# Two key batches loaded over the first feed-forward's hidden rows, and fewer, longer runs of attention work between the projection's matmuls

## The chip, the cores and the metric

The kernel runs on one NeuronCore of a Trainium2 chip. The metric is the time of one execution on the device, in microseconds (us). Engines run side by side, each in the order of its own program, and wait for each other on semaphores: TensorE (PE) multiplies matrices, VectorE (DVE) and ScalarE (ACT) work on elements, GpSimd (POOL) does a little, and SyncE (SP) issues nearly all DMA transfers from HBM.

## The reference

One inference step of a decoder layer for a prompt of 256 tokens and 8 samples of one token each with 1024 cached keys and values, all in fp32:

```python
x = x + 0.5 * swiglu_ffn(x, ffn1_norm, ffn1_w_in, ffn1_w_out)        # 1024 -> 2 x 2816 -> 1024
proj = rmsnorm(x, mix_norm) @ w_in                                    # u | q | k | v | q_mem, 2048 columns
y_pool = pool_mixer(u, ...)                                           # causal means of 2, 4, 8, 16 tokens
q, k = rotary(rmsnorm(q)), rotary(rmsnorm(k))                         # 8 heads x 64
y_moba = moba_attention(q, k_all, v_all)                              # blocks of 256: best 3 past ones and the own
y_mem  = mem_attention(rmsnorm(q_mem), mk, mv)                        # 4 heads, 256 memory tokens
x = x + concat(y_pool, y_moba, y_mem) @ w_out
x = x + 0.5 * swiglu_ffn(x, ffn2_norm, ffn2_w_in, ffn2_w_out)
```

The samples' keys and values lie in 128-token pages of a paged cache, found through `page_table`: 8 batches of 8 pages of 256 KB for the keys, and as many for the values.

## The kernel before

**Matmuls.** Every big product is split in high and low fp32r parts and done as three matmuls (`three`, L1504): L1506, L1507, L1508. For each weight tile of 512 KB SP loads `raw`, ACT writes the high part `w_hi` (L702), DVE the low part `w_lo` (L1022), and PE uses both. A ring of four such tiles turns: ACT's split of unit n waits until PE has used unit n - 4, and SP's load of unit n until DVE has split unit n - 4. The small products of the attention and all sample work are plain fp32 matmuls or PE transposes.

**The first feed-forward** ends with 22 units of `w_out` (`ffn_out(0)`, L1570): unit k takes hidden row k from `h_hi` and `h_lo`, which take 23 KB a partition each, and the last two units run together (`last_two`, L1599), so they wait for both splits. Meanwhile SP loads these units, the pages of key batch 3, and looks up the page numbers of batches 4 to 7 (`HELD`), 4 per unit at the end (L569 to L580). DVE, after each split, turns a pair of key pages in place (`turn_pair`, L1030): 16 pairs, those of batches 0 to 3, at the splits of units 6 to 21 (L1309). Then come the splits of the projection's units 0 and 1, the residual, and the samples' input `xs` (L1318).

**The projection rows.** The projection `x @ w_in` has 16 weight units, the rows r = 0 to 15: four each for q, k, v and for u with q_mem. Each row is four steps P (`project`, L1609) of three matmuls. All else up to the mixing product `w_out` is hung between the P by a table written by hand, `EXTRA` (L399): `EXTRA[r][i]` lists the tokens that come before the i-th P of row r, or behind it for i = 4; `TAIL` (L423) holds what follows the last row. PE, ACT, DVE all walk the same list (`steps`, L433) and each does its part of a token, so the list sets the order on all three. Tokens that matter here:

- S r: the samples' matmuls of row r from `raw` (L1638, 16 matmuls); ES their evacuation. ET: evacuation of the prompt's projection (`token_evac`).
- K b: the logits of key batch b (`key_logits`, L1653, 32 matmuls L1666). G g: DVE turns page pair g (four pairs a batch). QF: ACT spreads the queries of batches 4 to 7, after K3.
- OWN, A: own key and the softmax of the samples' logits; A3 holds its exponentials, A4 the turns of the probabilities, A5 the own values. V b: the values of batch b (L1940, 64 matmuls).
- NQ, NV, ND, NS, NG, NR: squares (ACT), variances (DVE), roots (ACT), scales, gains, rope (DVE) of a norm. T: turns of prompt queries and keys on PE (L1514) with ACT's evacuation.
- HA, HM, HE, HV, HB, HT, PV: logits, maxima (DVE), exponentials (ACT), scaling (DVE), turns (PE), evacuation (ACT) and values of the prompt's heads, two heads at a time for HA and PV. HY: evacuation of a pair of PV. MG: turns of memory key pages. Y, YR: turns and scaling of the samples' values. M, MK: the memory softmax and logits of the samples.
- W r, WL r: the splits of weight unit r on ACT and on DVE.

**Loads in the rows.** SP walks its own list (L599 to L631): projection units with key batch 4 behind unit 3, batch 5 behind unit 7, then 6, 7, the values, the memory keys and values, and the mixing weights. A batch goes to a slot as soon as the batch that had it is used (`free_wait`, L333). Batch 4 goes to `early_slot`, over the hidden rows, once the feed-forward is done (`w_used` at `U_WIN`).

Of the kernel before, what the change touches and what calls it, by code (L numbers as in the profile page):

```python
# [110 lines left out]
def layer(nc, a):  # L111

    ctx = ExitStack()
    with ctx:
# [99 lines left out]
        at[0] = late_end
        early_slot = place("early_slot", [P, PAGES * 512], at=at[0])
        vp = over("vp", [P, 2, 512])
        up = over("up", [P, 2, 512])
        kT = over("kT", [P, 4, NP])
        prob_pair = over("prob_pair", [P, 2, 2, NP])
        kp = over("kp", [P, 2, 512])  # L220
        probT_pair = [probT_even, over("probT_odd", [P, 2 * NP])]
# [12 lines left out]
        joined = over("joined", [P, 3, P])
        same, repeat, quarter_of = joined[:, 0, :], joined[:, 1, :], joined[:, 2, :]
        own_y = over("own_y", [P, 2, 4, 4])
        v_cols = over("v_cols", [P, P])
# [1763 lines left out]
```

## Time and profile before

| | us |
|---|---|
| median of 3 runs (lowest, highest) | 560.4 (559.86, 560.5) |
| the profiled execution | 560.33 |
| its span, first to last instruction | 558.5 |
| PE busy | 551.9 (99%) |
| DVE busy | 398.8 (71%) |
| ACT busy | 269.4 (48%) |

The stretches of the span that matter here: units 2 to 21 of the first feed-forward's second product end at 215.2 us, the projection rows reach to about 310, the tail to 337.7, and the mixing product and the second feed-forward follow. PE's granted clock is 1.00 of 2.4 GHz in all of them. Matmuls overlap in the pipeline: the start of one to the start of the next is what one costs, and "busy" hides small losses. A bracket behind a row of the timeline is the idle time of that engine ahead of it and the engine and line that ended it.

### The profile page before, as it was taken

The page shows a single profiled execution, that of the slowest core. Times are in us where ns is not written, and L with a number is a line of the kernel's source. Part 1 is how long each engine was busy: PE and PEld are TensorE (multiplying, and loading weights), DVE is VectorE, ACT ScalarE, POOL GpSimd, SP SyncE. Part 2 cuts the span into 40 slices and gives each one's busy share as a digit, 9 for nine tenths or more (in the row PEclk, how much of TensorE's full clock was granted, in tenths as well). Part 3 has the DMA queues.
Part 4 walks back from the last instruction along what each step waited for, and adds up shares of the span by engine and source line. Part 5 has one row for each costly group of instructions (what it writes and reads, how often), then busy time and mean ns, then how long its engine had stood idle before and what let it go on. Part 6 is the DMA issues. An engine that isn't in the chain of part 4 may idle for free.

```text
span 558.5 us, 13391 instructions
## 1 busy us (share of the span) xinstructions
PE 551.9 (99%) x5075; PEld 514.3 (92%) x5075; DVE 398.8 (71%) x715; ACT 269.4 (48%) x425; POOL 17.7 (3%) x24
## 2 busy tenths in 40 slices
PE   9999999999999999999999999999999999999997
PEld 9999999999899998566777779999999999999997
DVE  4686878885688877899936685689777777664444
ACT  6843465444543337344535885475444344433330
POOL 1000000000000003000000000140000000000000
PEclk9999999999999999999999999999999999999999
DMA  8799999784567664899999984567756666465523
GB/s 242 220 262 303 268 316 282 239 248 152 191 217 273 209 205 154 283 344 383 361 315 377 374 301 137 164 179 196 211 171 188 186 171 191 133 226 181 188 75 79
DMA packets 137480, 128.40 MB, mean 230 GB/s; under 512 B 10936, under 2 KB 108879, under 8 KB 137431
## 3 DMA queue, kind: packets, MB, share of 16 engines
q1 hardware_dynamic: 134703, 127.24, 72.6%
q10 hardware_dynamic: 2736, 0.61, 0.5%
q8 instruction: 26, 0.43, 0.3%
q14 instruction: 15, 0.12, 0.1%
HBM read 125.12 MB, written 2.83 MB: 229 GB/s over the span
## 4 chain that ended last, share of the span: by engine, by line
PE 83%; DVE 7%; DMA 5%; ACT 2%; issue 1%; SPq 1%; DVEq 0%; ACTq 0%
PE banks L1506 24%; PE banks L1507 24%; PE banks L1508 24%; DMA raw<-in_ffn_w_in 4%; PE banks L1666 3%; PE banks L1514 2%; PE banks L1940 2%; DVE w_lo L1022 2%; PE banks L1638 1%; PE banks L1867 1%; PE banks L1891 1%; DMA page_ids<-in_page_table 1%; DVE banks L1436 0%; DVE kp L1138 0%; ACT w_hi L702 0%
## 5 line engine op out<-in xcount | busy, mean ns | idle before, releaser
L702 ACT ACTIVATE w_hi<-raw 128x1024 fp32r<-128x1024 f32 x158 | 166.4, 1058 | 195.7 <-PE banks L1508 157.6
L1022 DVE TENSOR_TENSOR w_lo<-raw,w_hi 128x1024 fp32r<-128x1024 f32 x158 | 193.8, 1232 | 74.2 <-ACT w_hi L702 73.2
L1506 PE MATMUL banks<-x_hi,w_hi 128*128 128x264 f32 x752 | 214.1, 285 | 0.2 <-DVE h_tmp L1066 0.2
L1507 PE MATMUL banks<-x_lo,w_hi 128*128 128x264 f32 x752 | 213.0, 283 | 0.0
L1508 PE MATMUL banks<-x_hi,w_lo 128*128 128x264 f32 x752 | 213.0, 283 | 0.0
L1506 PEld LDWEIGHTS banks<-x_hi,w_hi 128*128 128x128 f32 x752 | 141.6, 188 | 0.8 <-issue 0.7
L1507 PEld LDWEIGHTS banks<-x_lo,w_hi 128*128 128x128 f32 x752 | 141.7, 188 | 0.0
L1508 PEld LDWEIGHTS banks<-x_hi,w_lo 128*128 128x128 f32 x752 | 141.0, 188 | 0.0
L1506 PE MATMUL banks<-h_hi,w_hi 128*128 (+1 forms) x352 | 100.2, 285 | 0.1
L1508 PE MATMUL banks<-h_hi,w_lo 128*128 (+1 forms) x352 | 100.1, 284 | 0.0
L1507 PE MATMUL banks<-h_lo,w_hi 128*128 (+1 forms) x352 | 100.0, 284 | 0.0
L1506 PEld LDWEIGHTS banks<-h_hi,w_hi 128*128 128x128 f32 x352 | 66.4, 189 | 0.3 <-ACT mem_kv L880 0.3
L1507 PEld LDWEIGHTS banks<-h_lo,w_hi 128*128 128x128 f32 x352 | 66.4, 189 | 0.0
L1508 PEld LDWEIGHTS banks<-h_hi,w_lo 128*128 128x128 f32 x352 | 66.3, 188 | 0.0
L1066 DVE TENSOR_TENSOR h_tmp<-banks,rstd 128x264 f32<-128x264 f32 x44 | 18.9, 429 | 22.6 <-PE banks L1508 22.6
L1033 DVE STREAM_TRANSPOSE kv<-kv 128x1024 f32<-128x1024 f32 x28 | 33.9, 1228 | 0.0
L1506 PE MATMUL banks<-w_hi,x_hi 128*128 128x512 f32 x64 | 28.0, 438 | 0.3 <-ACT qp L795 0.3
L727 ACT ACTIVATE sg<-sg 128x264 f32<-128x264 f32 x44 | 18.3, 415 | 16.4 <-DVE sg L1061 16.4
L1508 PE MATMUL banks<-w_hi,x_lo 128*128 128x512 f32 x64 | 25.3, 395 | 0.0
L1507 PE MATMUL banks<-w_lo,x_hi 128*128 128x512 f32 x64 | 25.2, 394 | 0.0
L1075 DVE TENSOR_TENSOR h_lo<-h_tmp,h_hi 128x264 f32 (+1 forms) x44 | 19.1, 433 | 3.6
L1071 DVE TENSOR_TENSOR h_tmp<-sg,h_tmp 128x264 f32<-128x264 f32 x44 | 19.0, 432 | 2.8 <-ACT sg L727 1.5
(287 smaller groups left out, 503.9 us busy)
## 6 DMA issues: line engine op xcount, KB each, us to landing
raw<-in_ffn_w_in SPq DMA_DIRECT2D x86, 512.0 KB, 4.8
raw<-in_ffn_w_out SPq DMA_DIRECT2D x44, 512.0 KB, 3.8
kv<-in_cache_k SPq DMA_DIRECT2D x56, 256.0 KB, 4.9
kv<-in_cache_v SPq DMA_DIRECT2D x48, 256.0 KB, 6.3
raw<-in_w_in SPq DMA_DIRECT2D x12, 512.0 KB, 5.7
late_slot<-in_cache_v SPq DMA_DIRECT2D x16, 256.0 KB, 5.3
raw<-in_w_out SPq DMA_DIRECT2D x8, 512.0 KB, 7.2
raw<-in_mem_w_kv SPq DMA_DIRECT2D x4, 512.0 KB, 3.5
```

What stands on the lines that cost most here:

```text
L702: act.activation(w_hi[:, n % RING, :], raw[:, n % RING, :], ACT.Copy).then_inc(hi_ready, 1)
L727: act.activation(sg[:, s, :], sg[:, s, :], ACT.Silu).then_inc(silu_ready, 1)
L1022: vec.tensor_tensor(w_lo[:, n % RING, :], raw[:, n % RING, :], w_hi[:, n % RING, :].bitcast(F32), ALU.subtract).then_inc(lo_ready, 1)
L1033: vec.transpose(key_pair(g), key_pair(g)).then_inc(k_turned8, 1)
L1066: vec.tensor_tensor(h_tmp[:, s, :], bank[b0 + 2 * s + 1][:, 0:N], rstd[:], ALU.mult).then_inc(gu_free, 1)
L1071: vec.tensor_tensor(h_tmp[:, s, :], sg[:, s, :], h_tmp[:, s, :], ALU.mult).then_inc(hm_ready, 1)
L1075: vec.tensor_tensor(h_lo[:, ds(c, 1), :].rearrange("p a n -> p (a n)"), h_tmp[:, s, :], h_hi[:, ds(c, 1), :].rearrange("p a n -> p (a n)") ...
L1506: pe.matmul(out, lhs[0], rhs[0], start=start, stop=False)
L1507: pe.matmul(out, lhs[0], rhs[1], start=False, stop=False)
L1508: return pe.matmul(out, lhs[1], rhs[0], start=False, stop=stop)
L1514: return pe.transpose(out, in_, ident[0:k, 0:k])
L1666: mm = pe.matmul(bank[LG_BANK][32 * hp:32 * hp + 32, half * NP:(half + 1) * NP], q_cols[:, c0:c0 + 32], keys[:, 4 * hp + c], start=(b4 == ...
```

## The change

Seven things change, and no arithmetic:

1. Key batches 4 and 5 (`HIDDEN`) load during the first feed-forward's second product, each page over hidden rows that PE is done with: at units 6, 8, ... 20 SP waits until PE has used two more units, looks up and loads one page of each. 16 pages that were loaded in the rows move here; the lookups of `HELD` (now 6 and 7) are halved and stand at units 18 to 21.
2. DVE turns three pairs ahead of the product (`LEAD_PAIRS`) and the pairs 3 to 23 at the splits of units 6 to 20 (`EARLY_PAIRS`), up to two at a split. The turns of 16 to 19 and 20 to 23 wait for the hidden pages. K0 now waits for all 24 pairs.
3. Batches 6 and 7 load into the slots of 0 and 1 and are turned together (G 24 to G 31 in rows 3 and 4).
4. Key logits, samples, own keys and values are gathered: K0 to K3 together; S4 to S7 with K4, K5; K6, K7 with S8 to S11; S12 to S15 with V3. The logits of a head pair come ahead of the values.
5. Values load in another order: batch 0 waits for K2, batch 1 for K3, batch 2 now stands ahead of unit 14. The mixing weights' first unit, which SP issues ahead of value batch 5, waits for S12 as before, and S12 is now in row 14.
6. `rows`, `rows_x` get a place of their own beside the squares' buffer, so A and N tokens pass each other in other orders: A3 now comes before ND4, NQ5 after HE7. The wait of T2 on K4 becomes a wait of T0 on K5.
7. In the tail WL16 moves behind HV7, and HB10, HB11 ahead of M1.

```diff
-HELD = (4, 5, 6, 7)
+HELD = (6, 7)
+HIDDEN = (4, 5)
+LEAD_PAIRS = (0, 1, 2)
+EARLY_PAIRS = ((3,), (4,), (5, 16), (6,), (7, 20), (8, 17), (9,), (10, 21), (11,), (12, 18), (13,), (14, 22), (15,), (19,), (23,), ())
...
-            if kind == "k" and b == 4:
-                eng.wait_ge(w_used, U_WIN)
-            elif kind == "k" and b > 4:
-                eng.wait_ge(k_used, b - 4)
+            if kind == "k":
+                eng.wait_ge(k_used, b - 5)
             elif kind == "v" and b < 5:
-                eng.wait_ge(k_used, (4, 6, 7, 8, 8)[b])
+                eng.wait_ge(k_used, (3, 4, 7, 8, 8)[b])
...
             for k in range(HT):
                 load_unit(U_OUT1, k, 0, ffn_out[0][:, k:k + 1, :])
+                if k >= 6 and k % 2 == 0:
+                    t = k // 2 - 3
+                    sp.wait_ge(w_used, U_OUT1 + 2 * t + 2)
+                    for b in HIDDEN:
+                        pages[b, t] = page_of(b, t)
+                        load_page("k", b, t)
...
-            load_batch("k", 4)
+            sp.wait_ge(w_used, U_WIN)
...
-            load_batch("k", 5)
+            load_batch("k", 6)
+            load_batch("k", 7)
             load_projection(8)
-            load_batch("k", 6)
             load_projection(9)
-            load_batch("k", 7)
             load_projection(10)
             load_batch("v", 0)
             load_projection(11)
+            load_batch("v", 1)
             load_projection(12)
-            load_batch("v", 1)
             load_projection(13)
+            load_batch("v", 2)
             load_projection(14)
             load_projection(15)
-            load_batch("v", 2)
...
-                    if k == 2:
-                        act.wait_ge(k_used, 5)
+                    if k == 0:
+                        act.wait_ge(k_used, 6)
...
-                kv_wait(vec, "k", g // 4, (g % 4 // 2,))
+                if g // 4 in HIDDEN:
+                    vec.wait_ge(hidden_loaded[g % 4], 16 * 2 * len(HIDDEN))
+                else:
+                    kv_wait(vec, "k", g // 4, (g % 4 // 2,))
...
+            for g in LEAD_PAIRS:
+                turn_pair(g)
             ffn_out_loop(0, 0, 1)
...
-                pe.wait_ge(k_turned8, 4 * (b + 1))
+                pe.wait_ge(k_turned8, 4 * (b + 1) if b in HELD else 4 * HELD[0])
```

The table's change, as the order in which PE meets it (P x n stands for n projection steps). Before:

```
Px4 T5 Px2 S0-3 Px3 QT0 Px3 QT2 SS0 P K0 K1 P K2 K3 P S4-7 Px3 K4 Px3 T0 P K5 P T1 Px5 S8 Px2 K6 Px2 S9 Px4 S10 K7 OWN1
Px2 S11 P A1 Px7 A4 Px2 S12 Px2 A5 T2 P T3 V0 P HA0 S13 V1 Px3 HB0 HB1 P PV0 V2 HA1 S14 Px3 V3 HB2 HB3 P S15 PV1 HA2 V4
P MG0 Y0 P MG1 HB4 HB5 P MG2 P | PV2 HA3 MG3 V5 T4 POOL0 MG4 HB6 HB7 MG5 PV3 MG6 HA4 POOL1 MG7 QT1 V6 HA5 HB8 HB9 MK0
V7 PV4 M1 HB10 HB11 Vmem Y1 PV5 MIX0 ...
```

After:

```
Px4 T5 Px2 S0-3 Px3 QT0 Px3 QT2 SS0 P K0-3 Px2 S4-7 K4 K5 Px8 T0 P T1 Px4 K6 K7 S8-11 OWN1 P A1 Px11 A4 Px7 T2 P T3 A5 P
HA0 V0 V1 Px3 HB0 HB1 P HA1 PV0 V2 Px4 HB2 HB3 P HA2 PV1 V3 S12-15 Px2 Y0 Px2 MG0 HB4 HB5 P MG1 P | MG2 PV2 V4 HA3 V5
MG3 T4 POOL0 MG4 HB6 HB7 MG5 PV3 MG6 HA4 POOL1 MG7 QT1 V6 HA5 HB8 HB9 MK0 V7 PV4 HB10 HB11 M1 Vmem Y1 PV5 MIX0 ...
```

On DVE the stretch that holds the turns of batches 6 and 7 becomes: WL6 G24 to G30 WL7 NR2 G31 NV2 NS2 NV3 NS3 WL8 NG3 WL9 OWN0 A0 OWN1 WL10 A2 NV4.

## Rows read from the trace of the kernel before

**Rows 1.** The page, part 4: who makes up the chain that ended last.

```profile
PE 83%; DVE 7%; DMA 5%; ACT 2%; issue 1%; SPq 1%; DVEq 0%; ACTq 0%
```

**Rows 2.** Stage windows: length, busy time of PE, PEld, DVE, ACT, POOL, clock, DMA share.

```profile
156.10:215.20 59.10, 59.10 (x488) 59.10 (x487) 47.83 (x58) 23.32 (x27) 0.00 (x0) 1.00 0.63 208
215.20:310.40 95.20, 93.93 (x1148) 66.60 (x1146) 73.36 (x184) 45.90 (x100) 5.95 (x7) 1.00 0.98 337
```

**Rows 3.** PE in order of time (start, length, line): a break for sample matmuls.

```profile
219.13 0.39 PE L1506 MATMUL banks<-w_hi,x_hi 128*128 128x512 f32 x1
...
219.92 1.93 PE L1638 MATMUL banks<-raw,xs 128*8 128x128 f32 x64
221.78 0.50 PE L1506 MATMUL banks<-w_hi,x_hi 128*128 128x512 f32 x1
222.12 0.39 PE L1507 MATMUL banks<-w_lo,x_hi 128*128 128x512 f32 x1
222.34 0.39 PE L1508 MATMUL banks<-w_hi,x_lo 128*128 128x512 f32 x1
```

**Rows 4.** PE in order of time: sample matmuls that hand over to key logits.

```profile
263.19 0.62 PE L1638 MATMUL banks<-raw,xs 128*8 128x128 f32 x16
263.63 1.91 PE L1666 MATMUL banks<-kv,q_cols 128*32 128x256 f32 x32
```

**Rows 5.** PE in order of time: a break of four transposes.

```profile
246.12 0.60 PE L1514 MATMUL banks<-ident,qp 128*128 128x128 f32 x4
246.47 0.48 PE L1506 MATMUL banks<-w_hi,x_hi 128*128 128x512 f32 x1
```

**Rows 6.** PE in order of time: four places in the rows where it waits.

```profile
239.83 0.40 PE L1508 MATMUL banks<-w_hi,x_lo 128*128 128x512 f32 x1
240.50 0.48 PE L1506 MATMUL banks<-w_hi,x_hi 128*128 128x512 f32 x1 [0.27 <-ACT qp L795]
...
277.89 0.40 PE L1508 MATMUL banks<-w_hi,x_lo 128*128 128x512 f32 x1
278.44 0.33 PE L1514 MATMUL banks<-ident,v 128*128 128x128 f32 x1 [0.16 <-DVE p_own L1411]
...
288.60 1.15 PE L1514 MATMUL banks<-ident,prob_pair 128*128 128x128 f32 x6
289.50 0.48 PE L1506 MATMUL banks<-w_hi,x_hi 128*128 128x512 f32 x1
...
307.36 0.66 PE L1514 MATMUL banks<-ident,kv 128*128 128x128 f32 x4 [0.58 <-ACT kv L723]
```

**Rows 7.** SP's queue in order of time: a unit, a page, batches of eight pages.

```profile
173.99 0.33 SPq L457 DMA_DIRECT2D raw<-in_ffn_w_out  x1
177.25 0.34 SPq L493 DMA_DIRECT2D kv<-in_cache_k  x1
...
238.71 4.08 SPq L493 DMA_DIRECT2D kv<-in_cache_k  x8
...
294.68 5.81 SPq L496 DMA_DIRECT2D kv<-in_cache_v  x8
```

**Rows 8.** DMA issues, 216 to 345 us: count, KB each, median us to landing.

```profile
kv<-in_cache_k SPq DMA_DIRECT2D x24, 256.0 KB, 5.0
raw<-in_w_in SPq DMA_DIRECT2D x8, 512.0 KB, 7.1
```

**Rows 9.** DMA issues, 150 to 216 us.

```profile
kv<-in_cache_k SPq DMA_DIRECT2D x8, 256.0 KB, 3.9
```

**Rows 10.** ACT in order of time: the split of `w_out` unit 21.

```profile
203.72 1.06 ACT L702 ACTIVATE w_hi<-raw 128x1024 fp32r<-128x1024 f32 x1 [1.85 <-PE banks L1508]
```

**Rows 11.** DVE in order of time: the split of unit 21, the last turn, `xs`.

```profile
204.82 1.22 DVE L1022 TENSOR_TENSOR w_lo<-raw,w_hi 128x1024 fp32r<-128x1024 f32 x1 [0.53 <-ACT w_hi L702]
205.96 1.24 DVE L1033 STREAM_TRANSPOSE kv<-kv 128x1024 f32<-128x1024 f32 x1
...
218.80 0.21 DVE L1318 TENSOR_TENSOR xs<-xT,gains 128x64 f32<-128x64 f32 x1
```

More of the change, by code:

```diff
@@ L57 @@
 ACT_PAGES = (0, 2, 4, 6)
-EARLY_PAIRS, AWAKE, AWAKE_2 = 16, 12, 3
+AWAKE, AWAKE_2 = 12, 3
 UNITS = 12
@@ L211, in layer @@
         x_wide = over("x_wide", [P, 3, P])
-        at[0] = region
+        slot_bytes, half_bytes = 4 * PAGES * 512, 4 * HT * N + 64
+        hidden_slots = [place(f"hidden_slot{i}", [P, PAGES * 512], at=region + i * half_bytes) for i in range(2)]
+        at[0] = region + slot_bytes
         qp = over("qp", [P, 2, 512])
[L214 to L221, printed above, removed]
+        joined = over("joined", [P, 3, P])
         q4 = over("q4", [P, P])
         k4 = over("k4", [P, P])
+        assert at[0] <= region + half_bytes
+        at[0] = region + slot_bytes
+        qmT = over("qmT", [P, 2, NP])
         v4 = over("v4", [P, P])
         u4 = over("u4", [P, P])
-        qm_cols = place("qm_cols", [P, 2, NS, 32], at=at[0])
-        qT = over("qT", [P, 4, NP])
-        qmT = over("qmT", [P, 2, NP])
+        v_cols = over("v_cols", [P, P])
+        ys = over("ys", [P, KT, NS])
+        own_y = over("own_y", [P, 2, 4, 4])
+        at[0] = region + half_bytes + slot_bytes
         mkT = over("mkT", [P, 2, NP])
+        probT_pair = [probT_even, over("probT_odd", [P, 2 * NP])]
         pm_cols = over("pm_cols", [P, 2, P])
-        ys = over("ys", [P, KT, NS])
+        sq_one = over("sq_one", [P, 1, P])
         stats = over("stats", [P, 80])
         m_stats = over("m_stats", [P, 4])
[L234 to L237, printed above, removed]
         marks = over("marks", [P, 8])
-        half_mark, two_mark = marks[:, 4:6], marks[:, 6:8]
-        sq_one = over("sq_one", [P, 1, P])
         own4 = over("own4", [P, 4])
@@ L247, in layer @@
         rm_pos = over("rm_pos", [P, 2 * CH])
+        same, repeat, quarter_of = joined[:, 0, :], joined[:, 1, :], joined[:, 2, :]
+        half_mark, two_mark = marks[:, 4:6], marks[:, 6:8]
+        at[0] = region + slot_bytes // 2
+        assert at[0] >= late_end
+        kp = over("kp", [P, 2, 512])
+        vp = over("vp", [P, 2, 512])
+        at[0] = region + half_bytes
+        qm_cols = place("qm_cols", [P, 2, NS, 32], at=at[0])
+        qT = over("qT", [P, 4, NP])
+        up = over("up", [P, 2, 512])
+        kT = over("kT", [P, 4, NP])
+        rows = place("rows", [P, 512], at=at[0])
+        rows_x = place("rows_x", [P, 512], at=at[0] + 4 * 512)
+        prob_pair = over("prob_pair", [P, 2, 2, NP])
         banks = ctx.enter_context(nc.psum_tensor("banks", [P, 8, 512], F32))
@@ L257, in layer @@
         raw_loaded = [sem(f"raw_loaded{i}") for i in range(RING)]
-        kv_loaded = [[sem(f"kv_loaded{i}_{h}") for h in range(2)] for i in range(KV_SLOTS + 2)]
+        kv_loaded = [[sem(f"kv_loaded{i}_{h}") for h in range(2)] for i in range(LATE_SLOT + 1)]
+        hidden_loaded = [sem(f"hidden_loaded{q}") for q in range(PAGES // 2)]
         pool_loaded = kv_loaded
@@ L490, in load_page @@
                     page = pages.pop((b, t))
-                done = kv_loaded[SLOT_OF[kind, b]][t // 4]
+                done = hidden_loaded[t // 2] if kind == "k" and b in HIDDEN else kv_loaded[SLOT_OF[kind, b]][t // 4]
                 if kind == "k":
```

18 lines of the change are left out of this document (8 added, 10 removed), and 42 rows, old and new, of tables (EXTRA, TAIL).

## The prediction

> **What bounds the kernel now.** I read the chain of work that ended last first: TensorE (PE) is 83% of it [rows 1], so time can be won only where PE loses it. The stage windows come next [rows 2]. In the second half of the first FFN PE issues 488 matmuls in 59.10 us, 0.121 us each, with nothing lost; a unit of 24 matmuls takes 2.91 us. The window of the projections, 215.20 to 310.40, is the one that the change reorders, and PE's work there in order of time shows where it leaks.
>
> *A break costs 0.30 us beside its own work.* A projection step P is three fp32r matmuls at a pitch of 0.22 to 0.23, 0.70 in all. In [rows 3] sample matmuls follow the P of 219.13 at 219.92: 0.79, so 0.09 going in. The 64 of them last 1.86; but 16 that hand over to other fp32 work last 0.44 [rows 4], so 64 should last 1.76: 0.10 coming out. The first pitch of the resumed P is 0.34 against 0.22 for the next: 0.11 more. Sum 0.30 for each change from P to fp32 work and back. A break that holds PE transposes alone goes in free (four take 0.35 [rows 5]) and costs some 0.09 on the resumed P.
>
> *Waits inside the stage.* In [rows 6] the P at 240.50 starts 0.67 after the matmul before it, 0.44 too late: a query evacuation which ScalarE (ACT) does behind the samples' one. The turn at 278.44 starts 0.55 after its predecessor, 0.32 late, for the own probabilities. Six probability turns at 288.60 take 0.90 until the next P, where six at the rate of [rows 5] take 0.53: 0.37 lost. At 307.36 PE waits 0.58 for a page's evacuation.
>
> **The change part by part.**
>
> *1. Shared runs.* By the order tables, PE leaves the P stream 30 times in the sixteen projection rows before and 22 times after. Full fp32 breaks go from 15 to 7 (left: S0-3; K0-3; S4-7 with K4, K5; K6, K7 with S8-11; HA0 with V0, V1; HA1, PV0, V2; HA2, PV1, V3, S12-15). 8 x 0.30 = **-2.4**. Two breaks that mixed fp32 work with turns lose it: V0 leaves the one with T3 (0.21 coming out) and V3 the one with HB2, HB3 (0.09 going in): **-0.3**. Two more breaks hold turns alone: 2 x 0.09 = **+0.2**. The matmuls stay the same in number and shape.
>
> *2. Waits that go.* At 240.50, K4 and K5 (3.5 us at the rate of [rows 4]'s second row) now stand between the samples and the next block's first P, so both evacuations fit under them: -0.44. The turn of 278.44 moves behind T2, a P and T3, 1.4 us later: -0.32. HB0 has V0, V1 and three P between its logits and itself (5.8 us) where S13, V1 and three P stood (4.5): -0.37. Together **-1.1**. The wait at 307.36 goes as well, but HB5 takes its place: the exponentials of head pair 2 now queue on ACT behind the samples' evacuation, which comes only after V3 and S12-15. I get 0.6 for it and put the pair at zero.
>
> *3. Waits that come.* K0 waits for all 24 early pairs; they end with the FFN, well before. T0 comes eight P (5.7 us) after K5. The rope that it needs stands on the vector engine (DVE) behind seven turns of batches 6 and 7, whose pages SP asks for when K0 and K1 are done. SP issues eight in 4.08 [rows 7], 16 in some 8.5; the last lands 5.0 later [rows 8]; G30, a split and the rope then end 0.3 us before T0. I take 0.1. The shared statistics (A1) have one P between the own-key matmul and themselves: 0.35. HA2 follows HB2, HB3 by one P and needs two evacuations of theirs: 0.2. Sum **+0.65**; bounds 0 (all just in time) and 2.4 (T0 alone 1.8 late, with the longest landing of [rows 8], 7.1).
>
> A rule speaks here. The same 256 KB key page lands in 3.9 when the stage moves less [rows 9] and in 5.0 in the projections [rows 8], where DMA is at a share of 0.98 [rows 2]. The Trainium skill (DMA: Bandwidth & Descriptors, Latency and other measured facts) gives an HBM access 0.2 us on average and 2 us at high load; the trace agrees in direction, with 1.1 us. By that rule a landing could still grow by 0.7 over the row, T0 would wait 0.4, and the sum would be 0.3 worse; by the row it is as above.
>
> *4. The end of the first FFN.* SP now carries 16 hidden pages with their lookups, DVE 24 turns instead of 16. A lookup is 0.59 (five of them between the unit issued at 173.99 in 0.33 and the page at 177.25 [rows 7]), a page with its lookup about 1.05. For units 9 to 16 SP then needs 2 x 0.4 + 4 x 1.05 = 5.0 of each 5.8 us, and the queues move 2.1 MB in it, 360 GB/s; at the 337 of [rows 2] that runs up 1.6 us over eight units, and the splits there end about 3 us before PE wants them. The tight spot is the end. PE releases the split of unit 21, so ends unit 17, at 203.72 [rows 10]; 2.91 a unit puts the end of unit 13 at 192.1 and of unit 19 at 209.5. At 192.1 SP starts: two pages 2.1, four lookups of held batches 2.3, unit 19, four lookups, unit 20, two pages. The last page is asked for at about 201.4 and lands 3.9 later [rows 9], at 205.3. Behind it on DVE are turn 19, split 20, turn 23 and split 21 at a pitch of 1.14 [rows 11]: split 21 ends at 209.9. PE takes units 20 and 21 together, at 209.5: 0.4 of wait. The projection's first two units follow SP's eight lookups, land at about 211 and put their splits, and the residual behind them, 1.6 later. The sample input, written from 218.80 on [rows 11], then comes at 220.6, while PE, 0.4 late itself, is there at 220.3: 0.4 with handover. **+0.8**; bounds 0 (pages land 1 us sooner) and 4.3 (rival 2).
>
> *5. Moves with one answer.* The three lead pairs fall before the split of unit 2, where DVE waits for ACT; without that gap they would cost 3.4. Value batch 5 is now asked for behind the mixing weights' first unit, which needs S12. From there to V5 PE has S13-15 (1.3), six P (4.4), Y0, MG0-2 and HB4, HB5 with their wait (2.7), PV2, V4, HA3 (3.5): 11.9 us; the pages need 0.4 + 5.8 to issue [rows 7] and about 5 to land: 11.2, covered by 0.7. V4 goes behind PV2, the same 1.8 us. Softmax rows in a place of their own, and T2's wait moved to T0, where six key batches are long done, cost nothing.
>
> *6. The tail.* The memory probabilities are turned behind HB10 and HB11; their evacuation then stands before the memory values: +0.4. The later split WL16 frees DVE for HV6, but NQ5, now behind the exponentials of pair 3, holds NV5 ahead of it: -0.1. **+0.3**.
>
> **Sum.** -2.4 - 0.3 + 0.2 - 1.1 + 0.65 + 0.8 + 0.3 = -1.85. The profiled execution took 560.33 us (span 558.5, 1.8 around it); the median of the runs is 560.4, which is the same within 0.1. 560.33 - 1.85 = 558.5. Laid out step by step, the new order came out a little shorter than the terms, since hand-overs inside a run go too; I say **558.4**.
>
> **The rivals.**
>
> *1. The gain is given back at T0: 560.2.* If the pages of batches 6 and 7 land like the projection's weights (7.1 [rows 8]), DVE stands still with a split and the rope behind, T0 waits 1.8, and all that follows moves by it. For: DMA share 0.98. Against: batch 4 no longer shares the stage, 2 MB less. Chance 0.20; the skill's rule above is its small beginning and within it.
>
> *2. Slower: hidden pages starve the last units, 561.9.* The place is SP's chain from unit 13 to 21. With a landing of 7.1 there as well, split 21 ends 3.2 later, PE stands 3.6 at the last two units, 0.4 at unit 16, and the sample input takes 0.3 more: 4.3 instead of 0.8. It makes the kernel slower by 0.2% from a landing of about 6.8. For: the kernel before loads no page there, and SP is serial. Against: the 3.9 of [rows 9] was measured with weights and pages in flight, and no page is issued behind unit 21. Chance 0.16.
>
> *3. Better: 556.7.* The waits of parts 3, 4 and 6 are all covered: -3.6. For: each is under 0.5 us and its cover is counted in whole instructions. Against: three independent places must all hold. Chance 0.20.
>
> **How the numbers follow.** Forecast 0.44, rivals 0.20, 0.16, 0.20. A measurement of this kernel can tell about 0.2%, 1.1 us, from no change, so faster is under 559.3 and slower over 561.5. Forecast and rival 3 are faster, 0.64; rival 1 is the same, 0.20; rival 2 slower, 0.16. The range reaches from just under rival 3, 556.3, to just short of rival 2, 561.3.
>
> **What would show it.** Right: the stretch from the first P to PV2 about 4.5 us shorter, 1.8 of it V4 that has moved behind; 128 key matmuls in one run; no wait at the second block's first P; a PE wait under 1 us at the last two units, with split 21 ending after 209. Wrong: PE waits over 1 us for DVE at T0, gaps in units 9 to 19, or a wait for a value batch in the tail.

## The result, and the profile after

The changed kernel takes 563.38 us, median of 5 runs (563.31 to 565.84), beside 560.4: a ratio of 1.0063, 95% interval 1.005 to 1.0077. It is slower by 3.0 us, where the prediction had it faster by 2.0, and it lies above the upper end of the predicted range, 561.3. The profiled execution took 563.33 with a span of 561.5. Line numbers are 9 to 19 higher than before.

The chain that ended last, by engine, in the kernel after (part 4 of the page; it answers to [rows 1]):

```profile
PE 83%; SPq 5%; DMA 4%; DVE 3%; ACT 2%; issue 2%; DVEq 0%
```

PE's share is the same, but SP's queue has gone from 1% to 5%: some of what PE does now hangs on when SP asks for something. The starts of the same instructions in both traces cut the span into stretches:

| us | before | after | change |
|---|---|---|---|
| start to the first P | 215.22 | 215.41 | +0.19 |
| first P to V5 | 97.46 | 95.52 | -1.94 |
| V5 to QT1 | 10.91 | 11.11 | +0.20 |
| QT1 to the mixing product | 14.14 | 18.67 | +4.53 |
| mixing product to the end | 220.77 | 220.79 | +0.02 |

So the rows gained and the tail lost more than twice as much. Of the signs that the prediction named for being wrong, two are there: a wait for DVE at T0, and one for a value batch in the tail. Of its signs for being right, the 128 key matmuls run together, the second block's first P does not wait, and PE waits 0.18 at the last two units; from the first P to PV2 it is 3.2 us shorter and not 4.5. What PE waited for in the kernel after (line, releaser: us in total, times, longest):

```profile
PE banks L1959 <- DMA kv<-in_cache_v: 3.3, 1, 3.3
PE banks L1533 <- DVE qp L1191: 1.8, 1, 1.8
...
PE banks L1947 <- ACT pm_cols L983: 0.5, 1, 0.5
PE banks L1657 <- DVE xs L1337: 0.4, 1, 0.4
```

The same in order of time (start, length, line; the bracket is the idle time ahead and who ended it):

```profile
220.55 1.93 PE L1657 MATMUL banks<-raw,xs 128*8 128x128 f32 x64 [0.38 <-DVE xs L1337]
...
250.73 0.66 PE L1533 MATMUL banks<-ident,qp 128*128 128x128 f32 x4 [1.84 <-DVE qp L1191]
...
310.93 1.94 PE L1959 MATMUL banks<-kv,p_cols 128*8 128x128 f32 x64
...
322.04 0.27 PE L1533 MATMUL banks<-ident,u 128*128 128x128 f32 x1
325.61 3.21 PE L1959 MATMUL banks<-kv,p_cols 128*8 128x128 f32 x64 [3.30 <-DMA kv<-in_cache_v]
328.75 1.13 PE L1886 MATMUL banks<-mkT,qmT 64*128 64x256 f32 x8
```

V5, the row of 310.93, does not wait. V6, the row of 325.61, stands 3.30 us for the pages of value batch 6, and then its 64 matmuls take 3.14 until the next row, where V5's take 1.86. That is the clock. Stretches of 1, 2 and 3 us around it in the kernel after (columns as in [rows 2]: busy times, then granted clock, DMA share, GB/s):

```profile
294.00:297.00 3.00, 3.00 (x39) 1.94 (x40) 0.00 (x0) 1.11 (x3) 0.00 (x0) 1.00 0.08 25
297.00:299.00 2.00, 2.00 (x84) 2.00 (x76) 1.58 (x4) 0.35 (x1) 0.00 (x0) 1.00 0.01 4
299.00:300.00 1.00, 1.00 (x46) 1.00 (x40) 0.93 (x5) 0.00 (x0) 0.00 (x0) 1.00 0.07 16
...
324.00:325.00 1.00, 0.00 (x0) 0.00 (x0) 0.90 (x5) 1.00 (x5) 0.00 (x0) 0.94 1.06 387
325.00:326.00 1.00, 0.39 (x9) 0.32 (x13) 0.82 (x4) 0.26 (x1) 0.00 (x0) 0.50 1.06 387
326.00:327.00 1.00, 1.00 (x26) 0.81 (x20) 0.00 (x0) 0.00 (x0) 0.00 (x0) 0.50 1.06 389
327.00:328.00 1.00, 1.00 (x28) 0.76 (x22) 0.00 (x0) 0.00 (x0) 0.00 (x0) 0.50 1.03 379
328.00:329.00 1.00, 1.00 (x26) 0.70 (x20) 0.00 (x0) 0.00 (x0) 0.00 (x0) 0.86 1.09 416
```

While PE stands, the granted clock falls from 1.00 to 0.50, 1.2 GHz, and comes back only some 3 us after the work has. V6 pays 3.14 - 1.86 = 1.28 for it. This is no accident of one execution: the mean granted clock is 0.994 to 0.997 in all five runs of the kernel after, and 0.999 or 1.000 in every run of the kernel before that stands beside the experiments. The first three lines hold the other half of the story: from 294 to 300, before all this, the DMA engines do next to nothing (shares 0.08, 0.01, 0.07), where the kernel before has 1.06 in the first of these stretches. SP's queue in the kernel after says why (start, length, what it issues):

```profile
231.28 9.33 SPq L502 DMA_DIRECT2D kv<-in_cache_k  x16
...
285.25 0.59 SPq L524 DMA_DIRECT2D kv<-in_cache_mem_k  x1
299.12 0.35 SPq L466 DMA_DIRECT2D raw<-in_w_out  x1
299.56 6.29 SPq L505 DMA_DIRECT2D kv<-in_cache_v  x8
...
307.06 5.39 SPq L466 DMA_DIRECT2D raw<-in_w_out  x1
312.54 6.31 SPq L505 DMA_DIRECT2D kv<-in_cache_v  x8
```

SP issues nothing for 13.3 us, from 285.84 to 299.12. It stands at the mixing weights' first unit, which waits for S12, and S12 now runs behind V3, at the head of the sample matmuls that start at 298.39. What SP's queue waited for has the same length (line, releaser: us in total, times, longest; L1657 are the sample matmuls):

```profile
SPq L465 <- PE banks L1657: 18.0, 2, 13.2
```

Then 7.9 MB must go through the queue up to V6's last page: three units of 0.52 MB, batches 5 and 6 of 2.1 MB each and the memory values' 2.1 MB. At the 387 GB/s that the last rows of the stretches show, that is 20 us from 299; from 300 to 306 the queues reach only 262, batch 7 takes a part beside it from 318.95 on, and batch 6 lands at 325.5. PE wants it at 322.2. The kernel before had the same loads in the same order (SP's queue, then V6):

```profile
290.27 4.30 SPq L457 DMA_DIRECT2D raw<-in_w_out  x1
...
308.99 6.28 SPq L496 DMA_DIRECT2D kv<-in_cache_v  x8
```

```profile
323.79 1.93 PE L1940 MATMUL banks<-kv,p_cols 128*8 128x128 f32 x64
```

The unit went out 8.85 us sooner there than now, and batch 6 3.55 sooner, so the queue made up more than half of the standing, but not all. Its last page was asked for at 314.7, and the longest landing of the eight was 7.7, so all of it was there by 322.4, at least 1.4 before V6. Now it is asked for 3.55 later, PE comes to V6 1.55 sooner, since the rows gained, and the longest landing is 7.3: 3.55 + 1.55 - 1.4 - 0.4 = 3.3, the wait. The Trainium skill (DMA: Bandwidth & Descriptors, Anatomy of one DMA — SWDGE (gpsimd) path) says that DMA engines wait for no semaphore, and that a wait happens at the issuing sequencer, ahead of the dispatch. The trace agrees: one unready unit kept back batch 5 and the memory values, 4.2 MB, which e3 below sends ahead of it.

### The profile page after: what moved, and what is told of

It reads as the page before. It is cut to its first block, busy times and chain, and to the rows that moved or that the text cites. A ratio compares the mean times of both kernels' runs of the same rounds, so it can differ in the third digit from the quotient of the medians.

```text
span 561.5 us, 13393 instructions
## 1 busy us (share of the span) xinstructions
PE 549.5 (98%) x5075; PEld 516.2 (92%) x5075; DVE 399.4 (71%) x715; ACT 271.3 (48%) x427; POOL 17.7 (3%) x24
## 3 DMA queue, kind: packets, MB, share of 16 engines
HBM read 125.12 MB, written 2.83 MB: 228 GB/s over the span
## 4 chain that ended last, share of the span: by engine, by line
PE 83%; SPq 5%; DMA 4%; DVE 3%; ACT 2%; issue 2%; DVEq 0%
PE banks L1525 24%; PE banks L1526 24%; PE banks L1527 24%; PE banks L1959 3%; PE banks L1533 2%; SPq L502 2%; SPq L487 2%; DMA kv<-in_cache_v 1%; DMA kv<-in_cache_k 1%; DMA raw<-in_ffn_w_in 1%; PE banks L1685 1%; SPq L505 1%; PE banks L1886 1%; DMA raw<-in_w_in 1%; PE banks L1910 1%
## 5 line engine op out<-in xcount | busy, mean ns | idle before, releaser
L1050 DVE STREAM_TRANSPOSE kv<-kv 128x1024 f32<-128x1024 f32 x24 | 29.1, 1230 | 5.5 <-DMA kv<-in_cache_k 5.5
```

Of the source, the lines that this page charges most:

```text
L1050: vec.transpose(key_pair(g), key_pair(g)).then_inc(k_turned8, 1)
```

## Experiments

Two questions were open: what starves V6 (the idle queue, or queues that are crowded anyway), and what T0's 1.8 us is worth. Each run is given by its median, that of the kernel before on the same chip, and the ratio over all runs with its 95% interval. Since a run starts up to 1 us earlier or later, stretches are compared from the first P on. A trace is one execution, and not always a middling one: those of e3 and e4 took 563.96 and 567.19, above the medians of 561.5 and 563.37.

**Value batch 5 into the idle stretch** (e1)

```diff
             load_memory("mk")
+            load_batch("v", 5)
             load_mix(0)
-            load_batch("v", 5)
             load_mix(1)
```

> Only the order on SP's list changes against the kernel after: value batch 5 is issued ahead of the mixing weights' first unit, which waits for S12. Theory (the idle queue): in the trace after SP stands from 285.8 to 299.1 at that unit, with the DMA share at 0.08 and less from 294 to 300, and all that is queued behind, value batch 6 the last of it that matters, lands late; PE then waits 3.3 us at V6 and runs V6 at half clock, 1.3 us more. Batch 5 in the idle stretch takes some 5.8 us of transfer out of the way: no wait at V6, clock 1.00 throughout, 563.4 - 3.4 - 1.3 = 558.7. Rival (the crowded queue): the 2 MB of memory values and the saturated queues ahead of batch 6 hold it wherever batch 5 stands; a wait over 1.5 us stays at V6, 561 or more.

It took 560.08 us beside 560.69, a ratio of 0.9993 (0.9978 to 1.0008). SP's queue and then PE at V6 in this run:

```profile
286.09 9.22 SPq L505 DMA_DIRECT2D kv<-in_cache_v  x8
300.15 0.83 SPq L466 DMA_DIRECT2D raw<-in_w_out  x2
...
305.94 5.48 SPq L505 DMA_DIRECT2D kv<-in_cache_v  x8
```

```profile
323.06 0.27 PE L1533 MATMUL banks<-ident,u 128*128 128x128 f32 x1
323.27 1.93 PE L1959 MATMUL banks<-kv,p_cols 128*8 128x128 f32 x64
```

Batch 6 is asked for 6.6 us sooner, V6 has no bracket, and the clock of this execution is 1.00 throughout. From the first P to the mixing product it takes 121.40, where the kernel after took 125.30 and the one before 122.51. The rival is out. The gain is 3.9, not 4.7: HA5 stops in its middle and loses 0.9, at the place where the kernel before loses 0.65; after, V6's wait had covered that. The time is 1.4 above the expected 558.7: 0.8 of it is this, and the rest fits another wait, 0.86 at the first P (below). Two of the twelve runs, 561.94 and 562.75, still have a mean clock of 0.996 and 0.997; they have no trace, so where it fell in them stays open.

**S12 back by two rows** (e8)

```diff
-            12: {1: [("HA", 0), ("V", 0), ("V", 1), ("HM", 0), ("HM", 1), ("HE", 0), ("HE", 1)], 3: [("HV", 0), ("HV", 1)], 4: [("HB", 0), ("HT", 0), ("HB", 1), ("HT", 1), ("WL", 14), ("W", 15)]},
+            12: {1: [("HA", 0), ("V", 0), ("V", 1), ("HM", 0), ("HM", 1), ("HE", 0), ("HE", 1), ("S", 12)], 3: [("HV", 0), ("HV", 1)], 4: [("HB", 0), ("HT", 0), ("HB", 1), ("HT", 1), ("WL", 14), ("W", 15)]},
...
-                 2: [("HA", 2), ("PV", 1), ("HY", 0), ("V", 3), ("S", 12), ("S", 13), ("S", 14), ("S", 15), ("ES", 3), ("YR", 0),
+                 2: [("HA", 2), ("PV", 1), ("HY", 0), ("V", 3), ("S", 13), ("S", 14), ("S", 15), ("ES", 3), ("YR", 0),
```

> Against the kernel after, one token moves on PE: the sample matmuls of row 12, S12, stand behind V1 in row 12 instead of behind V3 in row 14, and so the mixing weights' first unit and value batch 5 behind it can be asked for some 13 us sooner, with SP's list unchanged. Theory (S12's place is what starves V6): SP issues that unit at about 286, the wait at V6 and the half clock behind it go, and the stretch from the first P to the mixing product is 3.5 to 4.7 us shorter, as in e1. Rival (SP stands at the next unit, which waits for S13 behind V3, so the memory values and batch 6 are asked for no sooner): over 1.5 us of the wait stays.

It took 559.84 beside 560.33, a ratio of 1.0004 (0.9984 to 1.0023). SP's queue, then V6:

```profile
284.53 5.27 SPq L466 DMA_DIRECT2D raw<-in_w_out  x1
289.90 5.81 SPq L505 DMA_DIRECT2D kv<-in_cache_v  x8
...
304.84 5.49 SPq L505 DMA_DIRECT2D kv<-in_cache_v  x8
```

```profile
322.41 1.93 PE L1959 MATMUL banks<-kv,p_cols 128*8 128x128 f32 x64
```

V6 does not wait, the clock is 1.00, and from the first P to the mixing product it takes 120.84, 4.5 less than after. Nothing was changed on SP; one token on PE was enough. SP still stood at the second unit, for S13, as the rival said, but the 2.6 MB that went before it were what mattered. S12's place is what made V6 wait.

**V6 behind 3.9 us of PE's own work** (e4)

```diff
-                 ("QT", 1), ("V", 6), ("HV", 8), ("HV", 9), ("HA", 5), ("HM", 10), ("HM", 11), ("HY", 1), ("HB", 8), ("HT", 8),
-                 ("HB", 9), ("HT", 9), ("HE", 10), ("HE", 11), ("MK", 0), ("M", 0), ("V", 7), ("HV", 10), ("HV", 11), ("PV", 4), ("HB", 10), ("HB", 11), ("M", 1), ("W", 17),
+                 ("QT", 1), ("HV", 8), ("HV", 9), ("HA", 5), ("HM", 10), ("HM", 11), ("HY", 1), ("HB", 8), ("HT", 8),
+                 ("HB", 9), ("HT", 9), ("HE", 10), ("HE", 11), ("MK", 0), ("M", 0), ("V", 6), ("V", 7), ("HV", 10), ("HV", 11), ("PV", 4), ("HB", 10), ("HB", 11), ("M", 1), ("W", 17),
```

> Only the order of the tail changes against the kernel after: V6 goes behind HA5, HB8, HB9 and MK0, 3.9 us of PE's own work, on all engines. The loads are as late as before. Theory (the wait is for batch 6's last page alone, and the half clock follows PE's standing still): the work covers 3.3 us, PE does not stand, the clock stays at 1.00, 563.4 - 3.4 - 1.3 = 558.7. Rival (half clock is the stage's own, or V7 and the memory values land later in their turn): the clock falls in the tail all the same or a wait of over 1 us comes at V7 or at the memory values, 560 or more.

It took 563.37 beside 560.69, a ratio of 1.0043 (1.0029 to 1.0056). The expected 558.7 was missed. PE in the tail:

```profile
329.60 1.14 PE L1886 MATMUL banks<-mkT,qmT 64*128 64x256 f32 x8 [1.60 <-DVE kv L1042]
...
336.42 1.93 PE L1959 MATMUL banks<-late_slot,p_cols 128*8 128x128 f32 x64 [0.55 <-DMA late_slot<-in_cache_v]
```

V6 itself does not wait and the tail keeps its clock, but HA5, which came first now, stands 1.60 for the evacuation of the last memory page, and V7 0.55 for its own pages: QT1 to the mixing product is 16.82, so only 1.85 of the 4.53 came back. Another order in the tail only moved the wait to HA5 and V7; e1 and e8 remove it at its source. In this profile the wait at the first P was 2.10 and the one at T0 2.23, and each was followed by some 3 us at a granted clock of 0.50, so a part of the missing gain was lost there, ahead of the tail; of the other six runs four have a mean clock of 0.997.

**The rope ahead of the late page turns** (e2)

```diff
-            4: {0: [("NQ", 2), ("G", 27), ("G", 28), ("G", 29), ("G", 30), ("WL", 7)], 1: [("NR", 2), ("G", 31)], 3: [("NV", 2), ("NQ", 3)], 4: [("ND", 2), ("NS", 2)]},
+            4: {0: [("NQ", 2), ("G", 27), ("G", 28)], 1: [("NR", 2), ("WL", 7), ("G", 29), ("G", 30), ("G", 31)], 3: [("NV", 2), ("NQ", 3)], 4: [("ND", 2), ("NS", 2)]},
```

> Only DVE's order changes against the kernel after: the rope of the prompt's queries, NR2, goes ahead of WL7 and of the page turns G29 to G31. Theory: T0's wait of 1.8 us goes, since the rope then hangs on the query evacuation, which ends at 244.8, and not on the last page of batch 7; the chain from S12 to batch 6 moves with PE, so V6 waits 3.3 us as before: 563.4 - 1.8 = 561.6. Rival (the loss is only moved): batch 6's landing is set by the transfers of the stage before and not by S12, so V6 waits 5.1 us and the time stays at 563.4.

It took 564.91 beside 560.69, a ratio of 1.007 (1.0052 to 1.0088): no gain over after's 1.0063. What PE waited for:

```profile
PE banks L1959 <- DMA kv<-in_cache_v: 3.8, 1, 3.8
PE banks L1846 <- DVE own_by_half L1223: 1.3, 1, 1.3
...
PE banks L1916 <- DVE stats L1390: 0.6, 1, 0.6
```

T0's wait went, and 1.3 and 0.6 came at the next two places where PE needs DVE. Both theories put the loss in the wrong place: what is late is not T0 alone but DVE, and PE meets it again (V6 waits 3.8, not the rival's 5.1). DVE's order in the kernel after shows it:

```profile
237.26 2.37 DVE L1050 STREAM_TRANSPOSE kv<-kv 128x1024 f32<-128x1024 f32 x2 [2.92 <-DMA kv<-in_cache_k]
241.15 2.37 DVE L1050 STREAM_TRANSPOSE kv<-kv 128x1024 f32<-128x1024 f32 x2 [1.51 <-DMA kv<-in_cache_k]
243.86 2.37 DVE L1050 STREAM_TRANSPOSE kv<-kv 128x1024 f32<-128x1024 f32 x2 [0.34 <-DMA kv<-in_cache_k]
246.99 1.25 DVE L1050 STREAM_TRANSPOSE kv<-kv 128x1024 f32<-128x1024 f32 x1 [0.76 <-DMA kv<-in_cache_k]
248.16 1.18 DVE L1036 TENSOR_TENSOR w_lo<-raw,w_hi 128x1024 fp32r<-128x1024 f32 x1
249.26 0.89 DVE L1182 TENSOR_TENSOR rot<-qp,rope_q 128x128 f32<-128x128 f32 x4
```

The chain of waits through T0 (start, length, what) runs over the last page of batch 7:

```profile
240.27 6.69 DMA kv<-in_cache_k
```

DVE stands 5.5 us in all for pages that could not be asked for before K0 had freed their slot, and from 247 to the own keys at 260 it has hardly a gap. So what is put first there makes the rest later, as e2 shows.

**Both repairs, with the memory values early too** (e3; it has e2's edit, and this is what it adds)

```diff
             load_memory("mk")
+            load_batch("v", 5)
+            load_memory("mv")
             load_mix(0)
-            load_batch("v", 5)
             load_mix(1)
-            load_memory("mv")
             load_mix(2)
```

> Both repairs against the kernel after, with the memory values as well as value batch 5 ahead of the mixing weights' first unit, and the rope ahead of the late page turns. Theory: the losses are separate and add: 563.4 - 4.7 - 1.8 = 556.9, PE waits under 0.5 us everywhere in the projection rows and the tail, clock 1.00. Rival (crowded queue): the wait at V6 stays over 1.5 us, 559 or more. If the shared runs themselves brought nothing, the time would stop at that of the kernel before, 560.4.

It took 561.5 beside 560.69, a ratio of 1.0013 (0.9997 to 1.0029), and the expected 556.9 was missed. V6 does not wait, but the two waits of e2 at the own keys are there (1.31 and 0.64), this time followed by a clock of 0.50 from about 263.6 to 266.7, so that A1 to A4 takes 9.77 where it took 8.35 after. HA5 also stood 1.33 in its middle, for nothing that the profile names; what that was stays open. Neither theory saw this.

**SP's lookups out of the end of the feed-forward** (e5, against e1)

```diff
-                if k >= HT - 2 * len(HELD):
-                    for t in range(4):
-                        at_ = HELD[(k - HT + 2 * len(HELD)) // 2], k % 2 * 4 + t
-                        pages[at_] = page_of(*at_)
...
             for r in range(4):
                 load_projection(r)
+            for t in range(PAGES):
+                pages[HELD[0], t] = page_of(HELD[0], t)
             sp.wait_ge(w_used, U_WIN)
...
+            for t in range(PAGES):
+                pages[HELD[1], t] = page_of(HELD[1], t)
             for r in range(4, 8):
                 load_projection(r)
```

> Against e1_v5_first: the 16 page lookups of batches 6 and 7 move from SP's last units of the feed-forward behind its first four projection units. In e1 SP asks for those four units at 206.5, after eight lookups of 0.56 to 0.59 us, and the splits of the first two end at 214.9, so the first P waits 0.86 us and the sample matmuls 0.64. Theory (the end of the feed-forward hangs on SP's lookups): the units are asked for some 2 us sooner, both waits fall under 0.3 us together, first P at 215.3 or before, and the time is 1.0 to 1.3 us under e1. Rival (the landing of the two units, 4.8 to 6.9 us, depends on the chip and not on the request): waits of over 1 us in sum remain, time as e1.

It took 559.11 beside 560.33, a ratio of 0.9979 (0.9969 to 0.9989). The projection's first units on SP and the first P on PE in e1, then the units in e5:

```profile
206.49 3.44 SPq L466 DMA_DIRECT2D raw<-in_w_in  x4
```

```profile
216.62 0.47 PE L1525 MATMUL banks<-w_hi,x_hi 128*128 128x512 f32 x1 [0.86 <-DVE x_lo L1057]
```

```profile
202.63 7.16 SPq L466 DMA_DIRECT2D raw<-in_w_in  x4
```

Asked for 3.9 us sooner, they land in time: there is no wait at the first P, and the samples' matmuls start 4.69 behind it (5.49 in e1, 5.14 after, 4.70 before). The first P is at 216.52 and not at the expected 215.3, since this run's second product started 1.2 us later; from its first unit to the first P it takes 64.51, where e1 takes 65.79, the kernel after 64.94 and the one before 64.52. The rival had a point, though: in the profile of after the same wait is not to be seen, in e1 it is 0.86 and in e4 2.10, while the median landing of these units goes from 4.8 to 5.7 and 6.9. The late request cost anything from nothing to 2 us, as the landing fell.

**The own keys ahead of two splits** (e6, against e5: e2's edit, and WL8 behind OWN0, WL9 behind OWN1)

```diff
-            4: {0: [("NQ", 2), ("G", 27), ("G", 28), ("G", 29), ("G", 30), ("WL", 7)], 1: [("NR", 2), ("G", 31)], 3: [("NV", 2), ("NQ", 3)], 4: [("ND", 2), ("NS", 2)]},
-            5: {1: [("NV", 3), ("ND", 3)], 3: [("T", 0)], 4: [("T", 1), ("NS", 3), ("WL", 8)]},
-            6: {0: [("NG", 3)], 3: [("WL", 9)],
-                4: [("K", 6), ("K", 7), ("S", 8), ("S", 9), ("S", 10), ("S", 11), ("OWN", 0), ("A", 0), ("ES", 2), ("OWN", 1), ("WL", 10)]},
+            4: {0: [("NQ", 2), ("G", 27), ("G", 28)], 1: [("NR", 2), ("WL", 7), ("G", 29), ("G", 30), ("G", 31)], 3: [("NV", 2), ("NQ", 3)], 4: [("ND", 2), ("NS", 2)]},
+            5: {1: [("NV", 3), ("ND", 3)], 3: [("T", 0)], 4: [("T", 1), ("NS", 3)]},
+            6: {0: [("NG", 3)],
+                4: [("K", 6), ("K", 7), ("S", 8), ("S", 9), ("S", 10), ("S", 11), ("OWN", 0), ("WL", 8), ("A", 0), ("ES", 2), ("OWN", 1), ("WL", 9), ("WL", 10)]},
```

> Against e5_lookups_later: on DVE the rope goes ahead of WL7 and G29 to G31, as in e2, and the splits WL8 and WL9 go behind OWN0 and OWN1. In e2 T0's wait was gone, but 1.3 us came at the own keys and 0.6 at the shared statistics. Theory (DVE, held up 5.5 us by the late pages, is what PE waits for until the statistics, wherever it meets it): two splits less, 2.4 us, ahead of the own keys leave PE without a wait there too, T0 1.3 to 1.8 us better and nothing given back: 1.5 us under e5, about 557.5. Rival: the wait comes back at a split (WL8 at the first P of row 8) or at A1, time as e5.

It took 558.55 beside 560.33, a ratio of 0.9966 (0.9954 to 0.9978). Neither T0 nor the own keys wait, but 0.99 came at A1, for DVE, which had WL8 ahead of it:

```profile
260.70 0.41 PE L1916 MATMUL banks<-scratch,joined 128*128 128x64 f32 x2 [0.99 <-DVE stats L1390]
```

From the first P to the mixing product it takes 120.03 instead of e5's 120.31: the rival's way.

**And ahead of the statistics** (e9, against e6)

```diff
-                4: [("K", 6), ("K", 7), ("S", 8), ("S", 9), ("S", 10), ("S", 11), ("OWN", 0), ("WL", 8), ("A", 0), ("ES", 2), ("OWN", 1), ("WL", 9), ("WL", 10)]},
+                4: [("K", 6), ("K", 7), ("S", 8), ("S", 9), ("S", 10), ("S", 11), ("OWN", 0), ("A", 0), ("ES", 2), ("OWN", 1), ("WL", 8), ("WL", 9), ("WL", 10)]},
```

> Against e6_rope_own_first: the split WL8, which stood between OWN0 and A0 on DVE, goes behind OWN1. In e6 the first statistics (A1) waited 0.99 us for DVE, whose chain to them held that split of 1.2 us. Theory (DVE's chain to the statistics is still what PE meets): the wait at A1 falls under 0.2 us, the stretch from the first P to the mixing product goes from 120.0 to 119.1, 0.9 us less: 557.7. Rival: the first P of row 8 waits for WL8 instead, or the saving is taken up by a wait behind it, and the time is that of e6.

It took 556.64 beside 560.83, a ratio of 0.9925 (0.9913 to 0.9938). A1:

```profile
258.95 0.33 PE L1916 MATMUL banks<-scratch,joined 128*128 128x64 f32 x2
```

The wait at A1 is gone and none came for it; to the mixing product it takes 118.80, 1.2 less. With it goes T0's loss, for the first time without a new place. The time fell by more, 1.9 us; in the two profiles the other 0.9 lies ahead of the second product, which the edit does not touch, so only the 1.2 is its worth.

**Eight breaks more** (e7 against e6: K2, K3; K4, K5; K6; V0; V1; V2; S12, S13 and S14, S15 each apart, with a P between)

```diff
-            3: {0: [("WL", 5), ("NV", 1)], 1: [("K", 0), ("K", 1), ("K", 2), ("K", 3), ("ND", 1), ("NS", 1), ("QF", 1), ("WL", 6)],
-                3: [("S", 4), ("S", 5), ("S", 6), ("S", 7), ("ES", 1), ("ET", 0), ("K", 4), ("K", 5), ("G", 24), ("G", 25)], 4: [("ET", 1), ("G", 26)]},
+            3: {0: [("WL", 5), ("NV", 1)], 1: [("K", 0), ("K", 1), ("ND", 1), ("NS", 1), ("WL", 6)], 2: [("K", 2), ("K", 3), ("QF", 1)],
+                3: [("S", 4), ("S", 5), ("S", 6), ("S", 7), ("ES", 1), ("ET", 0), ("G", 24), ("G", 25)], 4: [("K", 4), ("K", 5), ("ET", 1), ("G", 26)]},
...
-            6: {0: [("NG", 3)],
-                4: [("K", 6), ("K", 7), ("S", 8), ("S", 9), ("S", 10), ("S", 11), ("OWN", 0), ("WL", 8), ("A", 0), ("ES", 2), ("OWN", 1), ("WL", 9), ("WL", 10)]},
+            6: {0: [("NG", 3)], 3: [("K", 6)],
+                4: [("K", 7), ("S", 8), ("S", 9), ("S", 10), ("S", 11), ("OWN", 0), ("WL", 8), ("A", 0), ("ES", 2), ("OWN", 1), ("WL", 9), ("WL", 10)]},
...
-            12: {1: [("HA", 0), ("V", 0), ("V", 1), ("HM", 0), ("HM", 1), ("HE", 0), ("HE", 1)], 3: [("HV", 0), ("HV", 1)], 4: [("HB", 0), ("HT", 0), ("HB", 1), ("HT", 1), ("WL", 14), ("W", 15)]},
-            13: {1: [("HA", 1), ("PV", 0), ("V", 2), ("HM", 2), ("HM", 3), ("HE", 2), ("HE", 3)], 3: [("HV", 2), ("HV", 3)], 4: [("WL", 15)]},
+            12: {1: [("HA", 0), ("HM", 0), ("HM", 1), ("HE", 0), ("HE", 1)], 2: [("V", 0)], 3: [("V", 1), ("HV", 0), ("HV", 1)], 4: [("HB", 0), ("HT", 0), ("HB", 1), ("HT", 1), ("WL", 14), ("W", 15)]},
+            13: {1: [("HA", 1), ("PV", 0), ("HM", 2), ("HM", 3), ("HE", 2), ("HE", 3)], 2: [("V", 2)], 3: [("HV", 2), ("HV", 3)], 4: [("WL", 15)]},
...
-                 2: [("HA", 2), ("PV", 1), ("HY", 0), ("V", 3), ("S", 12), ("S", 13), ("S", 14), ("S", 15), ("ES", 3), ("YR", 0),
-                     ("HM", 4), ("HM", 5), ("HE", 4), ("HE", 5)]},
+                 2: [("HA", 2), ("PV", 1), ("HY", 0), ("V", 3), ("HM", 4), ("HM", 5), ("HE", 4), ("HE", 5)], 3: [("S", 12), ("S", 13)], 4: [("S", 14), ("S", 15), ("ES", 3), ("YR", 0)]},
```

> Against e6_rope_own_first: eight changes between projection steps and other fp32 matmuls more: K2, K3 apart from K0, K1; K4, K5 apart from S7; K6 apart from K7; V0 and V1 each by itself; V2 apart from PV0; S12, S13 and S14, S15 each by themselves. No matmul more or less. Theory (0.30 us a change, as the prediction had it): the stretch from the first P to V5 is 2.4 us longer, waits for other engines set aside. Rival (a change costs only the 0.10 of the pipeline coming out): 0.8 us longer. If the shared runs were worth nothing: no difference.

It took 560.19 beside 560.33, a ratio of 0.9996 (0.9985 to 1.0007). V5 in e6, where the first P is at 215.91, and in e7, where it is at 215.18 and the lines are one less:

```profile
309.87 1.93 PE L1959 MATMUL banks<-kv,p_cols 128*8 128x128 f32 x64
```

```profile
311.30 1.93 PE L1958 MATMUL banks<-kv,p_cols 128*8 128x128 f32 x64
```

From the first P to V5 it takes 93.96 in e6 and 96.12 in e7. The waits in it are 1.61 in e6 (0.99, 0.28 and twice 0.17) and 1.68 in e7 (1.07 of them at Y0). Without them eight breaks cost 2.09, 0.26 each.

**The old order of the tail** (e10, against e9)

```diff
-                 ("HB", 9), ("HT", 9), ("HE", 10), ("HE", 11), ("MK", 0), ("M", 0), ("V", 7), ("HV", 10), ("HV", 11), ("PV", 4), ("HB", 10), ("HB", 11), ("M", 1), ("W", 17),
-                 ("M", 2), ("HT", 10), ("HT", 11), ("YR", 1), ("V", "mem"), ("WL", 17), ("Y", 1), ("PV", 5), ("HY", 2), ("W", 18), ("CAT", 0),
+                 ("HB", 9), ("HT", 9), ("HE", 10), ("HE", 11), ("MK", 0), ("M", 0), ("V", 7), ("HV", 10), ("HV", 11), ("PV", 4), ("M", 1), ("W", 17),
+                 ("HB", 10), ("HB", 11), ("M", 2), ("HT", 10), ("HT", 11), ("YR", 1), ("V", "mem"), ("WL", 17), ("Y", 1), ("PV", 5), ("HY", 2), ("W", 18), ("CAT", 0),
```

> Against e9_splits_behind: in the tail HB10 and HB11 go back behind M1, as in the kernel before, so that the memory probabilities are turned ahead of them and their evacuation is done before the memory values. Theory (part 6 of the prediction: the new order costs 0.4): the wait of 0.47 at the memory values goes, 0.4 us less than e9. Rival (M1 then waits for its exponentials, or HB10 is late in its turn): a wait of the same size comes at the turns, time as e9.

It took 556.48 beside 560.83, a ratio of 0.9922 (0.9909 to 0.9935). The memory values in e9 and in e10:

```profile
330.39 1.93 PE L1947 MATMUL banks<-kv,pm_cols 128*8 128x128 f32 x64 [0.47 <-ACT pm_cols L983]
```

```profile
330.12 1.93 PE L1947 MATMUL banks<-kv,pm_cols 128*8 128x128 f32 x64
```

The wait goes, and the stretch to the mixing product is 0.51 shorter (118.29). The times of e9 and e10 are too close to tell apart; the profile shows the step. e10, the change with five edits to its order, is 4.3 us faster than the kernel before, and 6.9 faster than the kernel after by the medians, 7.9 by the two ratios.

## Why the prediction was wrong

**Shared runs (-2.5): right.** The stretch from the first P to V5, less MG3's 0.58, which now stands behind V5, and less the 1.71 of waits in [rows 6], was 95.17. After, less 2.83 of waits (T0 1.84, S0 0.38, A4 0.27, the key turns and MG2 0.17 each), it is 92.69: -2.48. (Brackets are a little shorter than the loss from start to start; with the latter for T0 and S0 it is -2.7.) e7 puts a break at 0.26 where [rows 3] gave 0.30.

**Waits that go (-1.1): a little better.** All four of [rows 6] are gone, and HB5's, which was to take the place of the fourth, did not come: the turn of a memory page there waits 0.17.

**Waits that come (+0.65): T0 failed.** The samples' own steps were fine: A1 and HA2 do not wait, A4 waits 0.27. T0 waited 1.84 instead of 0.1 (1.3 to 2.2 in e1, e4, e5 and e8, which leave DVE's order as it is). The mechanism was the one described, and two terms of its sum were too small: SP asked for the last of the 16 pages 9.0 after the first, where 8.5 was counted, and it landed 6.7 after its request and not 5.0. That is 2.2 late, less the 0.3 that was to spare: 1.9. The row was right about the pages, whose median was 4.8 here, but DVE waits for the last of them, and that is not the median one. It is the first rival's wait, in its place and its size, though its landing of 7.1 came to only 6.7 and slower issuing made up the rest; the rival's total of 560.2 did not come, since V6's loss stands beside it. And T0 was only the first to meet a late DVE: e2, e6 and e9 together show that the loss is that of DVE's chain from the pages to the statistics.

**The end of the first feed-forward (+0.8): right in this profile, in part by luck.** It lost 0.42 up to the first P, counted from the second product's first unit (0.19 from the start of the span, since this run was 0.23 ahead by then), and 0.44 at the samples' matmuls: 0.86. The second rival did not come: PE waits at no unit before the last two. But five of the experiments have the same order up to there, and the same two losses come to 2.06 in e1, 1.68 in e2, 2.32 in e3, 4.13 in e4 (half clock included) and 0.65 in e8. What hung on SP's lookups was the projection's first units, and with a slower landing they cost up to 2.1 at the first P. The term has no such wait.

**Value batch 5 at no cost: the step that failed.** The sum for V5 itself held: its last page was asked for at 305.3 and the longest landing was 4.8, so V5 was covered by 0.8, where 0.7 was forecast. But the first mixing unit and batch 5 are not alone in SP's queue. The step followed the moved wait to one load behind it and stopped; V6, four transfers further, has its pages behind the memory values, and SP's queue made up only 5.3 of the 8.85 us by which the unit went out later, since the DMA engines, at a share of 1.06 from 306 to 324, had nothing to spare. A count like that for V5 would have shown how thin it was: 7.9 MB at 387 GB/s are 20 us from S12 on, with nothing lost at the start or to other loads, and PE needs 23 from there to V6. Nor did the sum ask what PE's own gain does to V6, which wants its pages 1.55 us sooner. It cost 3.4 of wait (from start to start, where the bracket has 3.30) and 1.28 of half clock, less 0.65 by which the kernel before waited at HA5 and which is hidden under it: 4.0 of the 4.85 between the sum of the terms, 558.48, and the profiled time. T0 is 1.7 of the rest, and the other terms, 0.9 better than forecast, make up the difference.

**The clock** was in no term. The sum priced every wait at its own length, and the 1.28 at V6 came on top.

**The tail (+0.3): right.** V5 to QT1, with MG3 where it was, is 0.38 shorter, and the memory values wait 0.47; e10 takes that away for 0.51.

## What to carry to other kernels

Where a step that a load waits for is moved later, walk the whole of the issuing queue behind that load, to the last transfer that can be late, in bytes against the rate of the stage, and against the new time at which it is wanted; here the first one behind it was covered and the fourth was not. Where an engine is late, look for the next place that needs it before moving one instruction ahead: the loss went from T0 to the own keys, to the statistics, and went away only when enough work had left the chain ahead of all three. And a wait can cost more than its length: behind those of 3.30, 2.23 and 2.10 us here PE worked at half clock for some 3 us.
